# Bias rows stored head by head, and four x tiles turned earlier, in a one-core transformer block

## The reference, cut to what matters

```python
def reference(x, p, rel_bias, g_mix, w_in, ...):
    bias_dsa, bias_swa = rel_bias[:, :DSA_HEADS], rel_bias[:, DSA_HEADS:]      # 4 and 8 heads, 32 buckets
    a = rms_norm(h, g_mix[i])
    (gq, gk, gv, gg, ga, dq, dk, dv, iq, ik, iw, sq, sk, sv) = jnp.split(a @ w_in[i], splits, axis=-1)
    o = jnp.concatenate([gla_mixer(...), dsa_mixer(dq, dk, dv, iq, ik, iw, bias_dsa),
                         swa_mixer(sq, sk, sv, swa_sinks[i], bias_swa)], axis=-1)
    h = h + o @ w_out[i]
    ...

# in dsa_mixer, for a block of 128 queries
rel = jax.nn.relu(jnp.einsum('bthd,bsd->bths', qib, k_idx))      # 8 index heads
score = jnp.einsum('bth,bths->bts', wb, rel).astype(f32)
score = jnp.where(admissible[None], score, -jnp.inf)
_, sel = lax.top_k(score, n_sel)                                 # the best 256 keys of each query
...
logits = jnp.einsum('bthd,btkd->bhtk', qb, kg) + bias            # bias by bucket of the distance
```

## Time and profile before

| what | us |
|---|---|
| median of three runs | 2824.75 (2823.98 to 2826.58) |
| the profiled execution, its own time | 2826.14 |
| its span, first to last instruction | 2824.4 |
| TensorE busy | 2588.1 (92%) |
| VectorE busy | 1860.8 (66%) |
| ScalarE busy | 1259.8 (45%) |
| GpSimd busy | 927.4 (33%) |
| mean granted clock of TensorE | 0.959 |

### The profile page before, as it was taken

The page is one execution under the profiler, slowest core; times in us unless marked ns, Lnnn a source line. Parts: engine busy times, 40 slices in busy tenths (PEclk is TensorE's granted clock), DMA queues, the critical chain, the costliest instruction groups (busy, mean ns, idle before and its releaser), DMA issues. The chain is left out here.

```text
span 2824.4 us, 35041 instructions
## 1 busy us (share of the span) xinstructions
PE 2588.1 (92%) x10908; PEld 1637.5 (58%) x10909; DVE 1860.8 (66%) x2646; ACT 1259.8 (45%) x2368; POOL 927.4 (33%) x925
## 2 busy tenths in 40 slices
PE   6999879999947889898899979999999999998998
PEld 3544424347823445444688756666666666665787
DVE  2389999979987788876333586644644444743676
ACT  2358667857956676766322222222222222222322
POOL 2377767810011111121000043434444444433221
PEclk9999989999967999999899989999999999999999
DMA  5202311122232223222544559975776665973663
GB/s 151 69 28 60 50 45 41 38 79 72 68 126 74 65 70 112 67 72 75 210 143 146 184 217 360 349 275 201 289 268 221 238 229 200 345 288 135 201 215 133
DMA packets 221475, 438.08 MB, mean 155 GB/s; under 512 B 22888, under 2 KB 91048, under 8 KB 221224
## 3 DMA queue, kind: packets, MB, share of 16 engines
q1 hardware_dynamic: 199400, 357.78, 36.9%
q0 software_dynamic: 13312, 47.32, 5.3%
q10 hardware_dynamic: 8640, 31.46, 2.8%
HBM read 331.14 MB, written 105.38 MB: 155 GB/s over the span
## 5 line engine op out<-in xcount | busy, mean ns | idle before, releaser
L2542 DVE CAST p_high<-p_low 128x2048 fp32r<-128x2048 f32 x128 | 203.2, 1587 | 400.8 <-PE p_psG L2649 293.0
L727 PE MATMUL p_psP<-home,p_ring 128*128 128x512 f32 x832 | 377.8, 604 | 11.3 <-DVE home L815 11.3
L2665 PE MATMUL p_psY<-p_wd,p_hT 128*128 x752 | 330.9, 593 | 2.2 <-ACT p_hT L2724 1.9
L2544 DVE TENSOR_TENSOR p_low<-p_low,p_high 128x2048 fp32r<-128x2048 f32 x128 | 318.9, 2492 | 4.4
L727 PEld LDWEIGHTS p_psP<-home,p_ring 128*128 128x128 f32 x832 | 153.8, 191 | 218.7 <-issue 206.1
L2665 PEld LDWEIGHTS p_psY<-p_wd,p_hT 128*128 128x128 f32 x752 | 139.3, 190 | 160.6 <-issue 160.5
L2585 POOL TENSOR_TENSOR p_xT_low<-p_xT,p_xT_high 128x512 fp32r<-128x512 f32 x94 | 186.0, 1997 | 3.3 <-ACT p_xT L2709 3.3
L2647 PE MATMUL p_psG<-p_high,p_xT_high 128*128 128x512 f32 x376 | 167.1, 444 | 15.7 <-DVE p_low L2544 8.0
L757 PE MATMUL p_psI<-p_kI,p_qI 64*128 64x512 f32 (+3 forms) x608 | 138.3, 574 | 27.7 <-ACT p_relu L618 26.2
L2591 POOL TENSOR_TENSOR p_hid<-p_act_g,p_act_u 128x512 f32<-128x512 f32 x47 | 62.1, 1321 | 308.2 <-ACT p_act_u L2719 295.3
L618 ACT ACTIVATE p_relu<-p_psI 128x1024 f32<-128x1024 f32 (+3 forms) x152 | 132.5, 914 | 64.3 <-PE p_psI L757 54.5
(11 more groups left out here) (423 smaller groups left out, 5848.4 us busy)
## 6 DMA issues: line engine op xcount, KB each, us to landing
p_low<-in_w_expert_gate_dram SPq DMA_DIRECT2D x32, 2048.0 KB, 13.3
p_low<-in_w_expert_up_dram SPq DMA_DIRECT2D x32, 2048.0 KB, 18.1
p_wd<-in_w_expert_down_dram SPq DMA_DIRECT2D x32, 2048.0 KB, 10.7
y_dram<-p_y ACTq DMA_DIRECT2D x47, 512.0 KB, 7.9
p_xt<-in_x_dram SPq DMA_DIRECT2D x32, 512.0 KB, 4.6
y_dram<-p_clear SPq DMA_DIRECT2D x32, 512.0 KB, 4.4
proj_f<-p_stage SPq DMA_DIRECT2D x52, 256.0 KB, 2.4
p_ot<-o_dram SPq DMA_DIRECT2D x16, 512.0 KB, 4.3
```

Of the source, the lines that this page charges most:

```text
L727: mm = pe.matmul(psP[0:n, i % 2, :], w, aT[:, k, c * CH:(c + 1) * CH], start=k == 0, stop=k == KD - 1)
L2542: dve.tensor_copy(high[:, m, k, :], low[:, par, m, k, :].bitcast(F32)).then_inc(high_done, 1)
L2544: dve.tensor_tensor(low[:, par, m, k, :], low[:, par, m, k, :].bitcast(F32), high[:, m, k, :].bitcast(F32), ALU.subtract).then_inc(w_split, 1)
L2665: mm = pe.matmul(psY[:, c, :], hT[:, k, :], wd[:, bass.ds(at, 1), k, c * CH:(c + 1) * CH].rearrange("p a f -> p (a f)"), start=k == 0, sto ...
```

## The change

The two stores of bias rows in front of product 36 become twelve, one a head, of one row each, and each is issued right behind the store of one of products 36 to 47. The semaphore `rows_stored` now counts to 16 times 12 instead of 32. SyncE's wait for the rows being filled stays in front of product 36.

The turning of x tiles 12 to 15 moves: on TensorE from in front of product 23 (`place[512, 2 * TPC]`) to in front of product 11, right behind score piece 7; on VectorE from in front of the search of group 1 to in front of that of group 0. The planner's 11 us for it move as well, from group 1 to group 0, and it sees the new order. The diff in full:

```diff
@@ -253,7 +253,7 @@
         for i in range(place["f", 0, 1], len(products)):
-            if i == place[512, 2 * TPC]:
+            if done == first_rel[4, 0] and ("X", 3) not in order:
                 order += [("X", 3)]
@@ -315,7 +315,7 @@
                     js = GROUPS[g]
-                    if (g, b) == (1, NBITS) and not late_x:
+                    if (g, b) == (0, NBITS) and not late_x:
                         late_x.append(True)
                         dve_at += 11.0
@@ -430,13 +430,15 @@
                 if p == ("f", 5, 0):
                     sp.wait_ge(filled, 2 + 2 * len(bucket_ranges()))
-                    for h0, n, rows in ((0, AH, rows_a), (AH, SH, rows_s)):
-                        sp.dma_start(bias_rows[h0:h0 + n, :, :], rows[:, :].unsqueeze(1).broadcast_to([n, P, 384])).then_inc(rows_stored, 16)
                 sp.wait_ge(copied, i + 1)
                 if p[0] == "f" and i in through:
                     r0, n = tiles[p[1]][0], tiles[p[1]][1][0][1]
                     q = through[i]
                     sp.dma_start(proj_f[r0:r0 + n, ts(p[2], CH)], stage[0:n, q % NSTAGE, :]).then_inc(stored[q % NSTAGE], 16)
+                    h = i - place["f", 5, 0]
+                    if 0 <= h < AH + SH:
+                        row = rows_a[h:h + 1, :] if h < AH else rows_s[h - AH:h - AH + 1, :]
+                        sp.dma_start(bias_rows[h:h + 1, :, :], row.unsqueeze(1).broadcast_to([1, P, 384])).then_inc(rows_stored, 16)
@@ -457,7 +459,7 @@
                     sp.wait_ge(first_masks, 16 * (MIDDLE - SCORED[0]))
-                    sp.wait_ge(rows_stored, 32)
+                    sp.wait_ge(rows_stored, 16 * (AH + SH))
@@ -939,7 +941,7 @@
             for g in range(len(GROUPS)):
-                if g == 1:
+                if g == 0:
                     turned_over(LAST_X, NT)
                 search(g)
```

## The result

| | before | after |
|---|---|---|
| median, us | 2825.44 (2823.98 to 2826.58, 4 runs) | 2800.20 (2799.59 to 2800.59, 4 runs) |
| ratio of the times | | 0.9911, 95% interval 0.9894 to 0.9928 |
| profiled execution, its span | 2826.14, 2824.4 | 2799.97, 2798.2 |
| TensorE, VectorE, ScalarE, GpSimd busy | 2588.1, 1860.8, 1259.8, 927.4 | 2583.8, 1854.6, 1259.8, 928.4 |
| mean granted clock | 0.959 | 0.964 |

A second set of runs of the changed kernel gave 2800.85 (2800.13 to 2802.11).

The account below looks back on a forecast made before the run. VectorE's bitwise searches, partly paced by products that ScalarE copies, were taken to bound the first part. Group 3's 16.2 or group 4's 16.8, plus 3 for GpSimd's adds, gave 19 us off: 2807, median 2806; range 2798 to 2815.

Parts of the forecast that it names:

- The stall: TensorE near 345 us: bias-row stores delay projection stores, leaving no score bank; 22.3 us lost, all to go.
- x turning: Last four x tiles turned behind score 7: 10.4 us on TensorE, only moved, so nothing over the whole.
- The first rival: Bias-row stores: a head goes at one row's pace, every 28 us instead of 11.1; 2980 us; 6%.
- the third: Stall near product 39 is hidden anyway or another wait replaces it; time stays 2822 to 2827; 5%.
- The second: VectorE becomes the pace: group 1 starts 6 us later than before; 15 off, 2811 us; 18%.
- group 1's start: VectorE's search of group 1 begins at 203.6, 2.5 us earlier; bounds 0.8 to 4.
- the term for GpSimd's adds: Group 2's select falls on block 12, slowing adds less; 0 to 7.3 us of TensorE's loss goes, 3 taken.
- the list's one-product shift: ScalarE's planned order puts one more product ahead of each shared bit, costing 6.9 of the 22.3 us.
- The fourth rival: All comes back: the one product's shift in ScalarE's order costs nothing; 24 to 27 off, 2799 us; 6%.
- the signs named: Trace marks: no TensorE hole at 345, x tiles turned at 113 to 123, group 1 near 203.6, heads under 8 us.
- The price of a head: One 192 KB bias-row store takes 1.7 to 7.6 us, hidden between products; 28 us as the far end.
- The 8.7 us limit: Stage slot is free if a head takes under 11.1 - 2.4 = 8.7 us, given a 2.4 us projection store.

Follow-up runs that it names:

- the bias rows alone: Kernel before with only the twelve one-row head stores; x tiles and ScalarE's order of copies and sign passes left as before: 2803.07 us, ratio 0.9924.
- the second execution: Another profiled execution of the unaltered changed kernel, with granted clock 1.00 in 116 to 122 us; group 1 to group 4's last bit came 1.4 us earlier.
- The kernel before with the select moved: Kernel before plus one wait, so VectorE begins group 2's select only when block 11 is masked: 2820.44 us, ratio 0.9981 to before.
- the x tiles alone: Kernel before with only the last four x tiles' turning and the planner's 11 us moved, the two old bias stores kept: 2832.12 us, ratio 1.0026.
- the old list: Changed kernel with ScalarE's order of copies and sign passes as planned for the x tiles' old place: 2797.74 us, ratio 0.9902 to before.
- all heads stored at once: Changed kernel with all twelve one-row stores issued ahead of product 36's store: 2844.99 us, ratio 1.0069 to before.

## Why the prediction came out as it did

**Right: the mechanism, and where it acts.** The stall came from the old stores and its 22.3 us went to the products in full: product 41 is 24.2 us earlier, which is 22.3 for the stall and 1.8 for a cheaper x turning, and the bias rows alone give 22.0 there. ScalarE has no wait for `proj_f<-p_stage` there any more, and TensorE runs at 1.00 clock through 340 to 360 us. SyncE, the weights and the wait at product 64 show no wait that TensorE or ScalarE would have passed on. By product 58 it is 30.8 us: 6.6 more, which came between products 41 and 47 and belong to GpSimd's adds near 400. In the second execution the x turning gives 3.2 instead of 1.8, product 58 is 32.2 earlier, and the 6.6 are the same. The kernel before with the select moved gave 6.7. The first rival (2980) and the third (stall hidden) are out by the result. The second is out by group 1's start; what it named, VectorE as the pace from bit 7 on, did come about, but because the products came early and not because VectorE was late.

**Mis-sized: the term for GpSimd's adds.** The forecast took 3 of 0 to 7.3 us; 6.6 came back. Its reason, that the select now falls on block 12 whose first round needs one add a piece, is the one that the traces show: an add of 3.07 us costs TensorE 0.57 us there, where one of 3.25 had stood beside a loss of 7.3. That the select beside the adds makes the loss was shown by itself in the kernel before; that it is one add instead of two that lets TensorE through was not tried separately.

**Mis-sized: the list's one-product shift.** "The 22.3 less one product of 6.9" is the step that failed. It holds only while products are the pace, as the x tiles alone show (6.6). Bit 7 was forecast to be due at 557.9, just when product 59 is copied; measured from piece 7 it was due 3.5 us earlier than that, and product 59 was there 8.5 us earlier than forecast and ahead of it by 5. So the shift cost 1.7 us in group 3 and 1.6 in group 4, shown by the run with the old list. The fourth rival said that it would cost nothing: its size (2799) was met, its reason only by half. A slip of 0.6 us stands beside it: the forecast lets bit 1 begin at 585.9 and ends bit 0 at 592.4, where two such bits take 7.1 in the trace of before (601.48 to 608.57), so 593.0.

**Mis-sized: group 1's start.** 2.5 us earlier was forecast, with 4 as the bound; it is 4.2 here, and 5.7 in the second execution and in the runs with x tiles alone and with the old list. TensorE's turning took 111.84 to 119.89, 8.05 us, and delayed the next product by 0.6: 8.65 instead of 10.4. In the second execution it took 7.3 and delayed nothing. How much less block 5's adds are stretched by group 0's select was halved by guess; nothing here measures it alone.

**Missing: shorter selects.** Bit 7 began 6.5 us earlier, and group 1's start and block 11's wait (0.5) make only 4.7 of it. The other 1.8 are the selects of groups 1 and 2, which took 13.9 and 18.5 us instead of 14.6 and 19.5. Their rows fall otherwise beside GpSimd's adds; with the bias rows alone, where group 1 starts as before, they took 13.4 and 18.1. The forecast had no term for this, and how much of it is chance of where an add lies is open.

**Put together.** Bit 7 began 6.5 us earlier instead of 3.0, and the shared bits took 30.06 us instead of 47.7, a gain of 17.6 where the forecast with all its terms had 16.2 (31.5, from 557.9 to 589.4). That is 24.1 for group 3 against a forecast of 19.2, and the 4.9 between them are 1.7 for group 1's start, 1.8 for the selects and 1.4 for the shared bits. At the part's end it is 24.9 against 19. So the stall and what it does to the products were right; that VectorE would set the pace from bit 7 on was not seen, and four terms were off, all in the same direction. That the result fell into the range is in part luck: only the fourth rival, given 6% and right by half in its reason, had put the range's lower end below it.

**Of the signs named.** Right: no hole at 345, x tiles at 112 to 121, bit 7 nearly without a wait on VectorE (0.20 us). Off: group 1 starts at 200.35, not 203.6; a head lands in 8.8 us, not under 8; the DMA share is high for 8 of each 11 us, not in short bursts; and there are waits in which ScalarE stands still for VectorE, which the text had listed as a sign against it, and which is how the larger gain looks.

**The price of a head.** The value of 1.7 us, from 7.1 GB/s an engine, was wrong, the other end (7.6, from the tail's 26 GB/s) nearly right: 7.2 us. The Trainium skill (SBUF — State Buffer, "Door 1: The DMA port swizzle") gave an estimated 7.2 us for one port's share, and the full queue shows 57.55 / 8 = 7.2. The Trainium skill's rule on the number of engines (DMA: Bandwidth & Descriptors, "Why a DMA increments its semaphore by 16 and not by 1") agrees with the trace as well, where the share is 0.81 to 0.84 of sixteen; but here the number of engines decided nothing of the rate. No run changed the partitions that a store reads, so that a port is what limits it is not shown by itself. The 8.7 us limit was drawn too simply: a head that lands in 8.8 us is over it and still costs nothing. The store of its own product is ahead of it in the queue, and the next one is issued 9.6 us behind it, when the head has landed.

## What to carry to other kernels

A gain that is passed on in full until another engine becomes the pace has no single price. The same shift of one product cost 6.6 us by group 3's last bit where products were the pace and 1.7 where they were not. Work out at which point the roles change, and look for the row in which the other engine begins to wait. When it has changed, look there for the next gain: after this change 7 to 10 us were to be had from VectorE's start and load, where before it the x move by itself made the kernel slower. A slow transfer needs room rather than speed: one each 11 us was hidden; twelve in a row made the kernel 20 us slower than before. And look at the granted clock before comparing two single profiles: the same kernel gave a group 1 start 1.4 us apart.

## What the runs showed of the hardware

A one-row store repeated 128 times (192 KB) keeps the sixteen DMA engines at a mean busy share of 0.81 to 0.84 and moves 26 to 27 GB/s in sum; the busy share is no measure of bytes moved.

VectorE and GpSimd slow each other, by the form of the instruction. In the kernel before, with the select beside adds, the comparison without a count takes 1.53 us for 896 columns, and the two passes that read two tensors 1.98 and 2.04 us:

```profile
386.19 1.98 DVE L916 SCALAR_TENSOR_TENSOR p_equal<-p_rank,p_need,p_equal 128x896 uint8<-128x896 f16 x1
388.20 2.04 DVE L918 SCALAR_TENSOR_TENSOR near<-near,p_flip,p_equal 128x896 uint8<-128x896 f32 x1
```

The same rows with all heads stored at once, where GpSimd stands still during the stall:

```profile
380.58 1.15 DVE L917 SCALAR_TENSOR_TENSOR p_equal<-p_rank,p_need,p_equal 128x896 uint8<-128x896 f16 x1
381.76 1.15 DVE L919 SCALAR_TENSOR_TENSOR near<-near,p_flip,p_equal 128x896 uint8<-128x896 f32 x1
```

The comparison takes 0.69 us there instead of 1.53; the counting pass of the same width takes 1.13 or 1.14 in both, and adds beside counting passes stay at 1.27. Not every pass is slowed: the scan of 896 columns (L914) takes 2.01 and 2.02, while the GpSimd add beside it in the kernel before took 2.97. The Trainium skill (SBUF — State Buffer, "Who interferes with whom") has it so: VectorE's two-input instructions and its `tensor_scalar` without an accumulator can hold ports that GpSimd needs, and counting forms do not. The rows named here agree, each seen in single executions.
